# The attention half of the output product moves from the mixing stage into the retrieval's preparation

## The reference, cut to what matters

```
proj = rmsnorm(x, norm_mix) @ w_in + b_in            # q 512 | k 128 | v 128 | u 512
attn = window_attention(q, k, v)                     # 512 wide, window 128, sinks
ssm  = s5_mixer(u, ...)                              # 512 wide, a scan over all tokens, GELU and GLU
mix  = concat(rmsnorm(attn, norm_attn_out), rmsnorm(ssm, norm_ssm_out))
x    = x + mix @ w_out                               # 1024 x 1024
q    = rmsnorm(x, norm_ffn) @ w_query                # 8 heads x 2 halves x 128
per head: top 16 of 128 keys in both halves, top 16 of their 256 sums -> idx; gate = softmax
act  = gelu(sum_d u_table[idx] * rmsnorm(x, norm_ffn))
x    = x + sum over 128 picks of gate * act * v_table[idx]
y    = rmsnorm(x, norm_final)
```

## Time and profile before

| what | value |
|---|---|
| median of three runs (lowest, highest) | 3240.16 us (3234.81, 3246.32) |
| span of the profiled execution | 3243.1 us, 28469 instructions |
| busy, share of span | PE 71%, DVE 66%, POOL 41%, ACT 29% |
| gather queue (1088 gathers) | 1142.99 MB, 86.1% of 16 engines' span |
| other queues | 63.21 MB, 5.6% |
| mixing | 0 to 284 us |
| scan and samples | 284 to 377.0 us |
| retrieval, up to the first gather (424.7 us) | 48 us |
| first tile (slots 0 to 127) | about 425 to 771 us |
| seven steady tiles and the samples | 771 us to the end |

### The profile page before, as it was taken

One profiled execution on the slowest core, in us unless ns is written; L12 is line 12 of the kernel. 1 busy time (PEld: TensorE's weight loads), 2 busy tenths in 40 slices (PEclk: granted clock), 3 DMA queues, 4 the chain that ended last, 5 costly groups with the idle time before them and its releaser, 6 DMA issues.

```text
span 3243.1 us, 28469 instructions
## 1 busy us (share of the span) xinstructions
PE 2290.3 (71%) x7579; PEld 785.6 (24%) x7579; DVE 2151.1 (66%) x5174; ACT 932.4 (29%) x3196; POOL 1345.1 (41%) x1266
## 2 busy tenths in 40 slices
PE   8998878766775667566756675667566766685676
PEld 4556543211221122111211121112111211121121
DVE  5546577787578657865686578656865686568654
ACT  2223244323222322232223222322232223222222
POOL 1232034444444444444444444444444444444442
PEclk9999988977787878688978797878788967796799
DMA  5224589999999999999999999999999999999998
GB/s 197 80 76 96 202 329 388 371 389 393 414 421 413 413 417 421 413 416 411 421 410 417 409 421 412 416 418 421 404 413 419 421 402 421 422 418 404 417 422 333
DMA packets 187986, 1208.01 MB, mean 372 GB/s; under 512 B 26600, under 2 KB 34328, under 8 KB 47360
## 3 DMA queue, kind: packets, MB, share of 16 engines
q0 software_dynamic: 157344, 1142.99, 86.1%
q1 hardware_dynamic: 30480, 63.21, 5.6%
HBM read 1190.30 MB, written 15.42 MB: 372 GB/s over the span
## 4 chain that ended last, share of the span: by engine, by line
DMA 32%; PE 24%; DVE 17%; issue 7%; ACT 5%; POOL 3%; DVEq 0%; POOLq 0%; ACTq 0%
DMA uv_ring<-in_uv_table,idx 32%; PE ACC L2128 15%; DVE uv_ring L1924 9%; PE ZS L2048 6%; POOL uv_ring L1551 3%; ACT dg L1696 2%; PE ZS L2023 1%; ACT dot L1689 1%; PE ZS L2009 1%; ACT dot L1676 1%; DVE idx_f L1846 1%; DVE S L1845 1%; DVE pos L1769 1%; DVE pos L1766 1%; PE ZS L2079 0%
## 5 line engine op out<-in xcount | busy, mean ns | idle before, releaser
L2128 PE MATMUL ACC<-uv_ring,dg 128*64 128x512 f32 x4352 | 1460.6, 782 | 903.2 <-ACT dg L1696 902.8
L1551 POOL DMA_INDIRECT uv_ring<-in_uv_table,idx x1088 | 1246.8, 1146 | 1549.2 <-PE ACC L2128 1317.1
L1924 DVE CUSTOM_DVE_ANT_0 uv_ring<-uv_ring,xn 128x1024 f32<-128x1024 f32 x1088 | 1326.7, 1226 | 733.5 <-DMA uv_ring<-in_uv_table,idx 699.4
L2128 PEld LDWEIGHTS ACC<-uv_ring,dg 128*64 128x64 f32 x4352 | 341.6, 165 | 1946.6 <-ACT dg L1696 1383.4
L1676 ACT ACTIVATE dot<-dot 128x2 f32<-128x2 f32 x544 | 110.6, 203 | 1880.8 <-DVE dot L1924 1880.8
L1696 ACT ACTIVATE dg<-stack,dot 128x64 f32<-128x64 f32 x1088 | 324.1, 340 | 17.7
L1689 ACT ACTIVATE dot<-gate,dot 128x1 f32<-128x1 f32 x1088 | 261.2, 287 | 18.9
L2048 PE MATMUL ZS<-score_w,xnT 128*128 128x512 f32 x512 | 246.2, 622 | 0.0
L521 PE MATMUL PJ<-w_in,xT 128*128 128x512 f32 (+1 forms) x384 | 141.0, 523 | 3.2 <-DVE pj L403 3.2
L2048 PEld LDWEIGHTS ZS<-score_w,xnT 128*128 128x128 f32 x512 | 94.6, 197 | 158.6 <-issue 158.6
L1924 DVE DVE_READ_ACCUMULATOR2_ANT dot<- 128x1 f32 x1088 | 89.0, 82 | 0.0
(11 more groups left out here) (355 smaller groups left out, 1609.4 us busy)
## 6 DMA issues: line engine op xcount, KB each, us to landing
uv_ring<-in_uv_table,idx POOLq DMA_INDIRECT x1088, 11.0
score_w<-in_w_query SPq DMA_DIRECT2D x8, 1024.0 KB, 18.9
w_in<-in_w_in SPq DMA_DIRECT2D x8, 640.0 KB, 9.0
xt<-in_x SPq DMA_DIRECT2D x9, 512.0 KB, 4.9
xr<-scratch_x SPq DMA_DIRECT2D x9, 512.0 KB, 8.4
xc<-in_x_columns SPq DMA_DIRECT2D x8, 512.0 KB, 3.9
out_y<-S SPq DMA_DIRECT2D x8, 512.0 KB, 7.8
scratch_u<-pj SPq DMA_DIRECT2D x9, 256.0 KB, 2.2
```

What stands on the lines that cost most here:

```text
L1551: pool.indirect_dma_start(out=ring[:, s_ % RING, :], out_offset=None, in_=a["uv_table"], in_offset=bass.IndirectOffsetOnAxis(ap=idx[:, s_: ...
L1924: V.tensor_tensor_reduce(row, row, xn[:, g, :], 1.0, 0.0, ALU.mult, ALU.add, dot[:, s_:s_ + 1]).then_inc(dots, 1)
L2128: ins = nc.tensor.matmul(ACCS[t % 2][GT * g:GT * (g + 1), b, :], dg[:, n % DG, :], ring[:, n % RING, D + 512 * b:D + 512 * b + 512], start ...
```

## The change

In the mixing, `mix`, `add_residual`, the residual loads and the `x1` stores go. In their place the turned attention `aT` is stored (256 KB a tile), after `take_attention`, which now waits until the last such store has landed. The roots of the attention stay in SBUF, in `early.rsa[:, t]`. `w_top` moves into `Early` and is loaded (2 MB) in the second stage. PE puts three matmuls of the u band of the next projection where `mix` was. DVE's `scale_columns` moves to the end of the step before. In the second stage the products of tile 7 and of the samples go, with their additions and stores; the sample attention is stored as two halves of 64 columns.

In the retrieval, SP loads `x` for `x1` and, new, `aT` into `z_and_cid`, once the mean square of y is taken. PE makes the top product in two halves (four matmuls each) at steps (1, 12) and (1, 14), for tile 0 at (0, 1) and (0, 2); DVE adds it to `xr` (two instructions) at (1, 15), for tile 0 at (0, 8). The bottom product waits for that addition, since it uses the same bank. For tile 0, z waits for it too. SP's loop is in a new order. `dynamic_dma_scratch_size=2048` is set. Smaller: the softmax of the gates works in place, and the first head's table lies inside `S`.

```diff
--- before.py
+++ after.py
@@ mix_tokens, SP
-                def load_residual(t, p):
-                    xk_in.held(sp, t - 1)
-                    xk_in.mark(sp.dma_start(xk[p][:], a["x"][bass.ts(t, P), :]))
-
-                def store_x1(t, p):
-                    k["x1_done"].held(sp, t)
-                    x1_out.mark(sp.dma_start(s["x1"][bass.ts(t, P), :], xk[p][:]))
+                def store_attention(t):
+                    k["aT_done"].held(sp, t)
+                    aT_out.held(sp, t - 1)
+                    aT_out.mark(sp.dma_start(s["aT"][bass.ts(t, P), :], aT[:].rearrange("p r n -> p (r n)")))
...
                     if not first:
-                        store_x1(t - 1, 1 - p)
-                        x1_out.held(sp, t - 1)
-                    if not last:
-                        load_residual(t + 1, 1 - p)
+                        store_attention(t - 1)
                     store_u(t + 1, 1 - p)
...
                 sp.dma_start(s["pj"], pj[0:NS_ROWS, 0, 0:U_COL]).then_inc(kept, 16)
+                store_attention(PT - 1)
...
@@ mix_tokens, DVE
                     k["weighed"].of(dve, t)
-                    dve.wait_ge(late, 16 * 2)
-                    k["mixed"].of(dve, t - 1)
+                    dve.wait_ge(late, 16)
+                    aT_out.of(dve, t - 1)
...
                     if not first:
                         take_attention(t - 1)
-                        scale_columns(t + 1, 1 - p)
                         if last:
                             par.input_matrices(nc, dve, 0)
                         mean_square(t - 1)
-                        add_residual(t - 1, 1 - p)
...
                     take_rest_of_u(t + 1, 1 - p)
+                    if not last:
+                        scale_columns(t + 2, p)
...
@@ mix_tokens, PE
                     if not first:
-                        mix(t - 1)
+                        project(t + 1, 2, range(0, 3))
                         sum_squares(t - 1)
...
-                        project(t + 1, 2, early)
+                        project(t + 1, 2, range(3, KD // 2))
...
@@ run_ssm_and_samples
                 early.load(sp, a)
+                early.load_top(sp, a)
...
-                sp.wait_ge(ev["x1"], 1)
-
-                for lo in (SEQ, SEQ + R):
-                    sp.dma_start(s["x1"][lo:lo + R, :], xr[:]).then_inc(stores, 16)
+                sp.wait_ge(ev["aT"], 1)
+                for lo in (0, R):
+                    sp.dma_start(s["aT"][SEQ:SEQ + P, :].rearrange("p (r n) -> p r n", n=P)[:, :, lo:lo + R], aT).then_inc(stores, 16)
...
-                shared.aT_done.of(pe, PT - 1)
-                for b in range(2):
-                    for r in range(REP):
-                        ins = nc.tensor.matmul(MO_7[:, b, :], shared.aT[:, r, :], w_top[:, r, 512 * b:512 * b + 512],
-                                               start=(r == 0), stop=(r == REP - 1))
-                ins.then_inc(ev["mixed_7"], 1)
...
@@ retrieve_experts, SP
-                    xr_in.mark(sp.dma_start(xr[:], s["x1"][bass.ts(t, P), :]))
+                    xr_in.mark(sp.dma_start(xr[:], a["x"][bass.ts(t, P), :]))
+
+                def load_attention(t):
+                    k["ms_y_done"].held(sp, t)
+                    aT_in.mark(sp.dma_start(z_and_cid[:], s["aT"][bass.ts(t, P), :]))
...
-                for t in range(PT - 1):
+                for t in range(PT):
                     load_xr(t + 1)
-                    load_y(t + 2)
-                    out(t, P)
-                load_xr(PT)
+                    load_attention(t + 1)
+                    if t > 0:
+                        out(t - 1, P)
+                    if t < PT - 1:
+                        load_y(t + 2)
+                    if t > 0:
+                        out_landed(t - 1)
...
@@ retrieve_experts, DVE
+                def add_attention(t):
+
+                    k["top_done"].of(dve, t)
+                    xr_in.of(dve, t)
+                    OP = product_bank(t)
+                    V.scalar_tensor_tensor(xr[:, 0:512], OP[:, 0, :], rsa[:, t:t + 1], xr[:, 0:512], ALU.mult, ALU.add)
+                    k["top_added"].mark(V.scalar_tensor_tensor(xr[:, 512:D], OP[:, 1, :], rsa[:, t:t + 1], xr[:, 512:D],
+                                                               ALU.mult, ALU.add))
...
-                    if at == (0, 13):
+                    if at == ((0, 8) if t == 0 else (1, 15)):
+                        add_attention(t)
+                    elif at == (0, 13):
...
@@ retrieve_experts, PE
-                    if at == (0, 4):
+                    if at in (((0, 1), (0, 2)) if t == 0 else ((1, 12), (1, 14))):
+                        b = int(at in ((0, 2), (1, 14)))
+                        if b == 0:
+                            aT_in.of(pe, t)
+                            k["xr_done"].of(pe, t - 1)
+                            if t == 0:
+                                pe.wait_ge(early.top_in, 16)
+                            else:
+                                k["zb_done"].of(pe, t)
+                        ins = product(t, b, aT, w_top)
+                        if b:
+                            k["top_done"].mark(ins)
+                    elif at == (0, 4):
...
                             pe.wait_ge(glu_in, 16)
+                            k["top_added"].of(pe, 0)
...
                         k["ynT_done"].of(pe, t)
-                        k["xr_done"].of(pe, t - 1)
-                        for n in range(SW // P):
-                            ins = nc.tensor.matmul(product_bank(t)[:, b, :], yT[:, n, :], w_bot[:, n, 512 * b:512 * b + 512],
-                                                   start=(n == 0), stop=(n == SW // P - 1))
+                        k["top_added"].of(pe, t)
+                        ins = product(t, b, yT, w_bot)
...
@@ kernel
-    nc = bacc.Bacc("TRN2", target_bir_lowering=False, num_devices=1)
+    nc = bacc.Bacc("TRN2", target_bir_lowering=False, num_devices=1, dynamic_dma_scratch_size=2048)
```

More of the change, by code:

```diff
@@ L139, in mix_tokens @@
         w_in = c.sb("w_in", [P, KD, IN_W])
-        w_top, g_attn, ident, half = shared.w_top, shared.g_attn, shared.ident, shared.half
+        g_attn, ident, half = shared.g_attn, shared.ident, shared.half
         b_in = c.sb("b_in", [P, IN_W])
@@ L267, in _ @@
                 sp.dma_start(g_attn[:], a["g_attn"]).then_inc(late, 16)
-                sp.dma_start(w_top[:], a["w_top"].rearrange("(k p) n -> p k n", p=P)).then_inc(late, 16)
-                load_residual(0, 0)
                 store_u(0, 0)
@@ L547, in sum_squares @@
                     k["summed"].mark(ins)
-                def mix(t):
-                    pe.wait_ge(late, 16 * 2)
-                    k["aT_done"].of(pe, t)
-                    k["pj_done"].of(pe, t + 1)
-                    for b in range(2):
-                        for j in range(AW // P):
-                            ins = nc.tensor.matmul(PJ[:, b, :], aT[:, j, :], w_top[:, j, 512 * b:512 * b + 512],
-                                                   start=(j == 0), stop=(j == AW // P - 1))
-                    k["mixed"].mark(ins)
                 def step(t, p, first, last):
@@ L577, in step @@
                     k["scored"].mark(ins)
-                    early = range(0, KD if first else KD // 2)
                     if not first:
-                        project(t + 1, 2, early)
+                        project(t + 1, 2, range(3, KD // 2))
                     project(t + 1, 0, range(KD))
@@ L836, in load, with load_top @@
             self.load_keys(sp, a, n)
+    def load_top(self, sp, a):
+        sp.dma_start(self.w_top[:], a["w_top"].rearrange("(k p) n -> p k n", p=P)).then_inc(self.top_in, 16)
 class Shared:
@@ L896, in run_ssm_and_samples @@
         mx, nm, sd, es, rs, den, rden = (small[:, i, :] for i in range(7))
-        ms, rstd = (stat[0:R, i:i + 1] for i in range(2))
-        ss_7, ms_7, rstd_7 = (stat_7[:, i:i + 1] for i in range(3))
-        x1_7, attention_7 = shared.xk_odd, shared.attention[:].rearrange("p i n -> p (i n)")
+        ms = stat[:, 0:1]
+        ss_7, ms_7 = (stat_7[:, i:i + 1] for i in range(2))
         PA = c.ps("PA", [P, 8, 512])
@@ L1181, in _ @@
                 tell(dve, "h_sample")
[L1183 removed]
+                dve.wait_ge(ev["squares"], 1)
                 ts(ms, XS, 1.0 / AW, EPS, ALU.mult, ALU.add).then_inc(ev["ms"], 1)
[L1185 to L1190 removed]
                 def take_outputs(n, i):
@@ L1341, in _ @@
                 pe.wait_ge(ev["one"], 1)
-                for r in range(REP):
-                    nc.tensor.matmul(XS, sqT[:, r, :], one[:], start=(r == 0), stop=(r == REP - 1))
-                for b in range(2):
+                pe.wait_ge(ev["summed_7"], 1)
+                for lo in (0, R):
                     for r in range(REP):
-                        ins = nc.tensor.matmul(MO[:, b, :], aT[:, r, :], w_top[:, r, 512 * b:512 * b + 512],
```

(14 more changed lines are left out.)

99 lines of the change are left out of this document (38 added, 61 removed).

## The result

The changed kernel took 3265.51 us (median of four runs, 3261.04 to 3270.73) against 3238.78 us (3234.81 to 3246.32) of the kernel before in the same comparison: ratio 1.0073, 95% interval 1.0059 to 1.0087. The forecast was 3240.0, within a range of 3208 to 3270. The time lies in the range, but the expected draw between savings and costs did not come: the sign is that of rival 2.

The account below looks back on a forecast made before the run. PE was taken to bound the mixing, the gather stream the steady retrieval. Terms -40.1 - 4.6 + 8.7 + 26 + 10 = 0.0 against the span of 3243.1, median 2.9 below: 3240, range 3208 to 3270.

Parts of the forecast that it names:

- rival 2: Steady tiles: DVE's wait at slot 15 costs more than the mixing gives, PE staying at half clock; 3270, chance 0.20.
- 1.5 of lateness is free: Steady tile, gather 30: landing 7.2 after issue against a shortest 5.7, so only 2.3 to 3.9 is lost.
- that wait goes: Second stage: DVE's wait of 1.81 behind the sample weighing vanishes with the removed products, L1170 ending at 352.1.
- Steady tiles: Retrieval, seven tiles: DVE's wait at slot 15 and aT's bytes cost 3.7 a tile, +26, bounds +4 and +56.
- Second stage: Tile 7's and the sample product leave PE, so the last outputs start earlier: -4.6, bounds -2 and -7.
- The mixing: Steps 1 to 7 without mix: 40.5 saved, less 0.4 for a store, -40.1, bounds -32 and -48.
- Start of the retrieval: aT load, eight matmuls and DVE's additions come before z, which ends 18.8 after the barrier: +8.7, bounds +6.5 and +12.
- First tile: Retrieval's first tile: DVE waits from about 546 to 558 for the addition at slot 41: +10, bounds +4 and +15.
- the runs' median lies 2.9 below: Whole kernel: the median of the runs was put 2.9 below the profiled span of 3243.1, giving 3240.
- Rival 1: Steady tiles: the ring swallows DVE's wait and only the bytes are paid, +5, first tile +5; 3214, chance 0.27.
- Rival 3: Mixing turns latency-bound, each step saving 4: mixing -28, total 3252, chance 0.10.
- rival 4: Retrieval: the small descriptor scratch throttles the gathers; 3630, chance 0.02.

Follow-up runs that it names:

- experiment 8: Changed kernel plus four unused matmuls on PE before the second stage's last outputs: 3265.97 us, a single run.
- experiment 7: Changed kernel with the load of w_top moved back into the mixing, behind g_attn: 3266.75 us, a single run.
- experiment 1: Changed kernel with the top product for tiles 1 to 8 at steps (1, 8) and (1, 10): 3232.09 us, ratio 0.9965 to the kernel before.
- experiment 4: Changed kernel with the top product for tiles 1 to 8 at steps (1, 10) and (1, 12): 3225.88 us, ratio 0.9952 to the kernel before.
- experiment 6: Kernel before with only the descriptor scratch set to 2048 bytes: 3246.58 us, ratio 0.9999.

## Why the prediction was wrong

Two terms failed: the price of a steady tile, in the step "1.5 of lateness is free", and the second stage, in the step "that wait goes" and in PE's clock, which it left at full. Term by term:

- *Steady tiles*, +26: this step failed. The wait was right and its price too small, 33.7 between the two profiled executions and up to 44 with the other traces. DVE waited 7.29 (forecast 8), and V of 16 and 17 began at 1481.15, 12.4 behind the end of DVE's slot 15; the forecast had it at 1489.9, 12.9 behind. That closeness is partly luck. The second half of the product was put in with 2.7 (1482.1 to 1484.8) though eight records of the earlier trace rows take half of 7.10, and took 3.70; V of 14 and 15 was taken at 3.63 and took 1.94. The chain was then followed on to gather 30, to be issued 3.8 to 5.4 late; it was issued 4.3 late. But "1.5 of lateness is free" held gather 30 against the shortest landing of all, 5.7, as if only it were late. Gathers 24 to 29 were late as well, so the queue in front of it did not get shorter: its landing was 7.2 from its issue before and 7.6 after, and 4.6 were lost where 3.1 were forecast. The sign named for this, landings of 5.7 to 6 around gathers 24 to 30, came only near gather 24 (6.3 in the median); at 26 to 30 they were 7.6 to 8.1. By segments the 4.8 a tile are 4.3 from slot 12 to 32, another 2.0 at the tile's edge (slots 112 to 8), which was not in the sum at all, and 1.5 less in slots 64 to 112.
- *Second stage*, -4.6: this step failed too, -0.5. It had two parts. "That wait goes" was false: DVE's wait behind the sample weighing is still 1.49, and L1134 starts 73.2 behind the last weighing, as L1170 did. PE's product of tile 7 did not cause it: with it gone, PE idles 5.88 in front of the samples' scores, released by DVE's copy of the keys. The other part, that the outputs start behind DVE's update and not behind the sample product, came true (75.7 behind the last weighing, 78.5 before), but the product had kept PE at full clock. Without it PE idled 3.80, and the first outputs ran at a granted clock of 0.50: 2.4 of 2.9 given back (experiment 8).
- *The mixing*, -40.1: right, the seven steps gave -39.7. Step 7 was mis-sized: it was forecast to save 3.9 and saved 2.2, since POOL's rotations became the wait. In front of the first step the trace shows +3.8, and executions of one and the same mixing differ by up to 3.4 there (last section).
- *The cover of the weights' load*, bound "late by up to 3": the y columns were late by 1.5 (experiment 7).
- *Start of the retrieval*, +8.7: 6.5. The attention landed 2.7 after SP's issue, where 2.2 was priced, but its issue was SP's first and not 1.1 behind it; the product took 9.94 for the 10.3 of the forecast; z ended 18.1 after SP's first issue, where 18.8 was said. Work behind z took back 1.5.
- *First tile*, +10: +9.9 between the two profiled executions. To hit it within 0.1 is luck, since the other traces of the two retrievals give 5.5 to 15. The wait of 11.62 was forecast as 12; that it makes all of the loss isn't shown, for in experiment 1 it is gone and the first tile still takes 352.7.
- *The sum against the median*: 0.0 was forecast and 16.1 came between the spans. Of the 26.7 between the medians, 10.6 lies in which executions were profiled. The step "the runs' median lies 2.9 below" treated the trace before as typical; later medians of the same kernel were 3243.65 to 3244.38, so that the level itself moves by 5 us between comparisons.
- *Rivals.* Rival 1 (the ring swallows DVE's wait) is wrong for 7.29 us and right for 2.52 (experiment 4). Rival 2 (slower) has the sign, and its 3270 is near the 3265.5 by luck: its cause, PE at half clock throughout, is not what happened, and the mean granted clock of 0.80 in the steady tiles before already spoke against it. Its own sum does not close either: 5.4 + 3 with nothing free is 8.4 a tile, not 7. In tile 3 the two top and the two bottom halves took 3.70 each and V between them 1.94, full clock for these shapes (granted 1.00 from 1466 to 1476); V of 16 and 17 was slow, 3.26 (granted 0.57 from 1480 to 1484), and so was V behind the `xr` block (0.50 from 1500 to 1504), but from 1484 to 1496 the clock was 1.00 in between, and gather 30 was issued 4.3 late, not over 8. So the rule of the Trainium skill, TensorE: Matmul & The Clock Gate, "What's actually happening" (throttled is the default, activity releases it), did not hold PE at half clock in the tiles, as rival 2 had it. In the second stage the trace agrees with it: the outputs ran at 0.50 after PE had idled 3.8. Rival 3 is out (periods as forecast), rival 4 by experiment 6.

## What to carry to other kernels

When work is put between the steps of a software pipeline, ask behind which queued instruction of its own engine its last part stands, and where the consumer's pair then begins: here two step numbers decided between +0.7% and -0.5% with identical instructions. The consumer's idle time is a poor price; follow the late operation to the first transfer that it holds up, and from there through all that follow: a slack read off one later transfer is only there if those in front of it are in time. And work taken off an engine ahead of a critical group can take the clock with it.

## What the runs showed of the hardware that was not expected

The granted clock at the start differs from execution to execution. The same sixteen records of the first projection, behind the same gap of 3.22 us, took 7.11, 10.01 and 8.52 us in three executions, with a granted clock of 1.00, 0.70 and 0.82 around them (29 to 37, 30 to 41, 31 to 40 us). Timelines of PE: before, changed, and before with the small scratch.

```profile
29.81 7.11 PE L521 MATMUL PJ<-w_in,xT 128*128 128x512 f32 x16 [3.22 <-DVE pj L403]
```

```profile
30.74 10.01 PE L502 MATMUL PJ<-w_in,xT 128*128 128x512 f32 x16 [3.22 <-DVE pj L395]
```

```profile
31.34 8.52 PE L521 MATMUL PJ<-w_in,xT 128*128 128x512 f32 x16 [3.22 <-DVE pj L403]
```

The first weighing came at 54.0 in the kernel before and at 57.0 in it with the small scratch, and at 54.5 to 57.8 in the seven traces of the changed kernel and its variants whose mixing is the same; every period behind it was the same to 0.1. So a shift of 3.4 us, as large as the terms of the sum, comes without any edit of the mixing.

An issue on SP can be held for microseconds by other transfers: 4.23 for 16 rows of y columns with 2 MB of weights asked for shortly before, 0.73 without them (experiment 7).
